# Forming a gating tile on VectorE instead of ScalarE in the mixing stage of a hybrid retention / SSD / MoE layer

## The reference

```python
def step(s, inp):
    xc, ac, bc, cc = inp                     # xc already holds dt * x
    acum = jnp.cumsum(ac, axis=1)
    seg = acum[:, :, None] - acum[:, None, :]
    lmat = jnp.exp(jnp.where(mask[None, :, :, None, None], seg, -jnp.inf))
    cb = jnp.einsum('bngs,bmgs->bgnm', cc, bc)
    y_in = jnp.einsum('bgnm,bnmgr,bmgrp->bngrp', cb, lmat, xc)
```

## Time and profile before

| | us |
|---|---|
| median of three runs (2853.01 to 2857.82) | 2855.8 |
| the profiled execution | 2853.01 |
| its span, first to last instruction | 2851.3 |
| TensorE busy in the span | 2332.4 |
| VectorE busy | 1407.6 |
| ScalarE busy | 1058.9 |
| GpSimd busy | 579.5 |

### The profile page before, as it was taken

One profiled execution on the slowest core, in us unless ns is written; L12 is line 12 of the kernel. 1 busy time (PEld: TensorE's weight loads), 2 busy tenths in 40 slices (PEclk: granted clock), 3 DMA queues, 4 the chain that ended last, 5 costly groups with the idle time before them and its releaser, 6 DMA issues. The chain is left out here.

```text
span 2851.3 us, 36459 instructions
## 1 busy us (share of the span) xinstructions
PE 2332.4 (82%) x11872; PEld 1917.0 (67%) x11873; DVE 1407.6 (49%) x1540; ACT 1058.9 (37%) x1471; POOL 579.5 (20%) x610
## 2 busy tenths in 40 slices
PE   4899989999994736787769991599999999999850
PEld 2688878999994315666658870477777777777740
DVE  2333331100102876788864444066566656546858
ACT  2333333222221220333322221166566656546732
POOL 0000000000001335677720014110010000000126
PEclk8899998999986869899989995699999999999985
DMA  7222241121115758544423433378696877658969
GB/s 257 70 89 88 88 151 64 45 89 44 45 62 169 293 198 306 212 157 162 162 84 140 147 117 98 118 261 292 226 319 240 279 266 248 222 201 292 362 223 372
DMA packets 296543, 517.35 MB, mean 181 GB/s; under 512 B 35248, under 2 KB 209456, under 8 KB 292272
## 3 DMA queue, kind: packets, MB, share of 16 engines
q1 hardware_dynamic: 261168, 394.52, 40.4%
q0 software_dynamic: 19200, 63.49, 6.4%
q10 hardware_dynamic: 16128, 58.73, 5.1%
HBM read 407.99 MB, written 108.69 MB: 181 GB/s over the span
## 5 line engine op out<-in xcount | busy, mean ns | idle before, releaser
L2107 DVE TENSOR_TENSOR e_w_low<-e_w_whole,e_w_high 128x2048 fp32r<-128x2048 f32 x186 | 417.9, 2288 | 128.8 <-ACT e_w_high L2060 128.8
L2060 ACT ACTIVATE e_w_high<-e_w_whole 128x2048 fp32r<-128x2048 f32 x186 | 345.5, 1908 | 44.8 <-DVE e_y L2125 44.8
L2013 PE MATMUL e_pG<-e_w_high,e_xT 128*128 128x512 f32 x768 | 305.3, 398 | 1.2 <-ACT e_xT L2053 1.2
L2014 PE MATMUL e_pG<-e_w_low,e_xT 128*128 128x512 f32 x768 | 305.5, 398 | 0.0
L602 PE MATMUL proj_acc<-w_high,hT_high 128*128 128x512 f32 x672 | 272.9, 406 | 6.9 <-DVE hT_low L637 5.7
L602 PE MATMUL proj_acc<-w_low,hT_high 128*128 128x512 f32 x672 | 268.7, 400 | 0.0
L602 PE MATMUL proj_acc<-w_high,hT_low 128*128 128x512 f32 x672 | 268.1, 399 | 0.0
L2032 PE MATMUL e_pY<-e_w_high,e_hT 128*128 128x512 f32 x768 | 226.0, 407 | 0.0
L2017 PE MATMUL e_pG<-e_w_high,e_xT 128*128 128x512 f32 x768 | 194.6, 395 | 0.0
L2013 PEld LDWEIGHTS e_pG<-e_w_high,e_xT 128*128 128x128 f32 x768 | 145.3, 189 | 36.6 <-issue 1.6
L2014 PEld LDWEIGHTS e_pG<-e_w_low,e_xT 128*128 128x128 f32 x768 | 145.4, 189 | 35.4
(11 more groups left out here) (286 smaller groups left out, 4509.5 us busy)
## 6 DMA issues: line engine op xcount, KB each, us to landing
e_w_whole<-in_moe_w_gate_dram SPq DMA_DIRECT2D x64, 1024.0 KB, 7.4
e_w_whole<-in_moe_w_up_dram SPq DMA_DIRECT2D x64, 1024.0 KB, 10.7
e_w_whole<-in_moe_w_down_dram SPq DMA_DIRECT2D x64, 1024.0 KB, 7.5
rows_done<-e_y ACTq DMA_DIRECT2D x48, 512.0 KB, 6.5
m_tok<-by_token SPq DMA_DIRECT2D x16, 1280.0 KB, 7.0
xt<-in_x_dram SPq DMA_DIRECT2D x32, 512.0 KB, 5.7
wm_rest<-in_w_mod_dram POOLq DMA_DIRECT2D x8, 2048.0 KB, 12.7
by_token<-tok SPq DMA_DIRECT2D x16, 768.0 KB, 5.6
```

The source lines that it names most:

```text
L2013: nc.tensor.matmul(pG[:, half], xT[:, 0, k], wh[:, half, w], start=(k == 0), stop=False)
L2014: nc.tensor.matmul(pG[:, half], xT[:, 0, k], wl[:, half, w], start=False, stop=False)
L2060: nc.scalar.activation(wh[:, third, part], raw[:, third, part], ACT.Copy).then_inc(whs.sem, 1)
L2107: nc.vector.tensor_tensor(wl[:, third, part], raw[:, third, part], wh[:, third, part].bitcast(F32), ALU.subtract).then_inc(wls.sem, 1)
```

## The change

The eight instructions that form `G` leave ScalarE and go to VectorE. On ScalarE each was an activation with a scale and a bias for each partition; on VectorE each is a `tensor_scalar`, multiply and add, with the same two operands. They stand behind `sT` (L1463) and ahead of the SSD output of tile t (L1467). The wait that ScalarE had for L1409 of the tile before falls away, since writer and reader are now on one engine in order. The counter `spreads` is gone; `gate` now counts three reports for each tile, the filling of `G` first.

```diff
-        spreads = kit.counter("m_steps_spread", 1)
-        gate = kit.counter("m_decays_gated", 2, credit=2)
+        gate = kit.counter("m_steps_spread", 3, credit=3)
...
-            def steps(t):
-
-                act.wait_ge(gate.sem, gate.at(t - 1, 1))
-                for h in range(SH):
-                    m = nc.scalar.activation(G[:, h], g["tri"][:, 0], ACT.Identity,
-                                             scale=g["dd"][:, bass.ds(t + NCT, 1), 0, h:h + 1].rearrange("p a b -> p (a b)"),
-                                             bias=g["dd"][:, bass.ds(t + NCT, 1), 1, h:h + 1].rearrange("p a b -> p (a b)"))
-                m.then_inc(spreads.sem, 1)
-
             def body(t, use, s):
                 if there(t + 1):
-                    steps(t + 1)
...
-                    dve.wait_ge(spreads.sem, spreads.at(t))
+                    dve.wait_ge(gate.sem, gate.at(t, 1))
                     dve.wait_ge(exps.sem, exps.at(t))
                     nc.vector.tensor_tensor(L[:], L[:], G[:], ALU.mult).then_inc(gate.sem, 1)
-                    dve.wait_ge(gate.sem, gate.at(t, 1))
+                    dve.wait_ge(gate.sem, gate.at(t, 2))
...
                     nc.vector.tensor_tensor(sT[:], bank[:, 4], g["DT"][:].rearrange("p h n -> p (h n)"), ALU.mult).then_inc(sTs.sem, 1)
+
+                    for h in range(SH):
+                        m = nc.vector.tensor_scalar(G[:, h], g["tri"][:, 0], g["dd"][:, bass.ds(tile, 1), 0, h:h + 1].rearrange("p a b -> p (a b)"),
+                                                    g["dd"][:, bass.ds(tile, 1), 1, h:h + 1].rearrange("p a b -> p (a b)"), ALU.mult, ALU.add)
+                    m.then_inc(gate.sem, 1)
```

## The result

The changed kernel takes 2875.8 us (median of four runs, 2873.1 to 2877.6) against 2854.9 (2853.0 to 2857.8): ratio 1.0069, 95% interval 1.0054 to 1.0084. It is slower by 20.9 us. The forecast was 2881, slower, with a range of 2862 to 2892.

The account below looks back on a forecast made before the run. The mixing loop was held to be bound by a cycle through the m_tok load, with VectorE idle at L1431. Adding 13.9, 9.9 and 2.2 us to 2853.0 gave 2879.0; the forecast was 2881, range 2862 to 2892.

Parts of the forecast that it names:

- The ring: Mixing loop: POOL's gate L1255, next loads, TensorE's transposes and L1317, VectorE's L1431, next L1255; 18.44 us a round.
- the spare: VectorE's idle time at L1431, behind load and TensorE: 40.1 us over 14 turns, 2.48 each in eleven.
- The removal at 0: Taking the eight activations, 3.19 us, off ScalarE gains 0, since nothing in the loop's cycle waits for them.
- The walk through the port: VectorE and POOL take turns on SBUF: the eight's 1.66 us of work becomes 3.82 us of delay up to L1409.
- The sum: Mixing loop's added time: 13.9 us up to L1431, 9.9 behind it, 2.2 in the last tile; 26.0 in all.
- first legs: From L1255's end to L1431, 10.84 us in the turn shown: 1.26 longer in eleven turns, 13.9 us.
- second legs: From L1431 to the next L1255's end: 8.31 us instead of 7.60, 0.71 in 14 turns, 9.9 us.
- long turns: Three loop turns with waits of 4.52, 4.16 and 4.11 us at L1431, said to lose nothing up to L1431.
- The port is not lost: Rival: the eight run in one go, 1.66 us; only the last tile pays, +2 us, 2855 to 2860; chance 0.12.
- Faster: Rival: the tile's store starts later, so m_tok lands 0.8 to 1 us sooner; 11 us gained, 2845; chance 0.05.
- Half of it: Rival: one POOL instruction misses the eight, or the way from L1431 does not stretch; 2862 to 2872; chance 0.18.
- More: Rival: two per-partition numbers make each instruction dearer, +0.3 to 0.8 us a turn; 2886 to 2895; chance 0.12.

Follow-up runs that it names:

- second execution: The kernel before, profiled again without any edit: 2854.7 us in a single run, loop 297.5 us.
- the half fill: The changed kernel with heads 0 to 3 of G on ScalarE and 4 to 7 on VectorE: 2862.3 us, ratio 1.0013 to the kernel before.
- the PSUM run: The changed kernel with the eight reading PSUM instead of SBUF, so G differs: 2839.0 us with one block of expert rows fewer; loop 298.9 against 316.4.
- the last experiment: The changed kernel with the eight moved into VectorE's idle stretch, behind L1426 and ahead of L1431: 2876.9 us, ratio 1.0077 to the kernel before.

## Why the prediction was right, and what was off

**The ring and the spare** held. Taking the load out of it gives back 33 us before, and nothing of the loop after.

**The removal at 0** held: 0.9994.

**The walk through the port** held to a quarter of a microsecond. It gave the eight 5.69 us (1.67 to 7.36), measured 5.93; L1409's end at 8.91 behind the gate, measured 9.13 (1272.19 + 1.21 − 1264.27); L1431 at 12.1, measured 12.1 to 12.2 in all fourteen turns. The order of the four waits was as written: the second to fifth of the eight take 1.06, 1.08, 1.08 and 1.93 us, the other four 0.33 to 0.34. The step was the small error: two per-partition numbers make 0.33 and 0.25 a step, not 0.29 and 0.207 (eight without company take 2.13 us for the first tile). Most of it hid behind POOL.

**The sum** of the loop against the first execution: first legs 14.2 us for 13.9 (14 x 12.21 = 170.9, before 156.8); second legs 9.9 for 9.9 (8.26 against 7.55 on average); the last tile 2.5 for 2.2 (its first leg 8.07 before, 10.53 after). 26.5 for 26.0. There is a little luck in the 14.2: the eleven short turns lost 15.2 and not 13.9, because L1409's end moved by 4.04 and not by 3.82, and the three long ones, which were to lose nothing, came out 1.0 shorter, since the changed kernel has no long turns. The stretch of the second leg, called one of the weakest steps, came out as the first tile had shown it.

**Where the 5 us between 26.5 and 20.9 lie** is in part open. The term that I hold to be off is the one for the long turns: the sum took their number, three, from one profile. The second execution of the kernel before has six and a loop of 297.5, so the change adds 18.9 to that one and 26.5 to the first. The changed kernel's loop is 316.4 and 316.5 in two profiles, since it no longer waits for what varies. One estimate speaks for a usual loop near that of the second execution: the half fill, whose turns are all alike, has a loop of 301.9 and runs some 4 us above the kernel before, which puts the latter's loop at 297 or 298. It is not shown: two profiles do not say how often long turns come, and the stretch ahead of the loop varies by 12 us by itself. I had also put the long turns down to the load alone; most of their length is TensorE's clock behind the wait.

**The rivals.** "The port is not lost" falls by the rows of the turn and by the PSUM run. "Faster" falls: the store now is issued 4.9 us later (8.2 us behind the gate instead of 3.3) and lands in 2.7 us instead of 7.0, but `m_tok` lands in 6.8 instead of 7.0, so 0.2 was there, not 0.8. "Half of it" did not happen. Its price for a turn without the `dav`, 8 to 12 us left in all, was too high: the run without it shows none (at most 2.3 by its interval). "More" was right that each instruction is dearer and wrong on how little of that hides: 0.24 us of a turn, not 0.3 to 0.8; its own terms give 2886 to 2893, not 2895. The Trainium skill's figure of 0.127 us for such an instruction (VectorE: DVE Perf Modes, TRN2 errata) is about half of the 0.25 step here. The Trainium skill's rule of the exclusive lock (SBUF — State Buffer, Who interferes with whom) agrees with the waits for `dav`, `kd`, `xd` and the decayed states in every run, and with the PSUM run; it does not with POOL's root of 4 columns in the last experiment, during whose 1.03 us VectorE's instructions ran at 0.34.

## What to carry to other kernels

Before giving VectorE work on SBUF, look at what GpSimd does in that stretch, not at VectorE's idle time: here a run of short instructions let each waiting large GpSimd instruction in between, and 2.13 us of work took 5.93. Reading PSUM avoided it even though each instruction got dearer. And where one engine has spare time because a ring passes through a load, try shortening the ring before filling the spare: here that was worth 33 us.

## What the runs showed of the hardware that I had not expected

- POOL gets the port between two VectorE instructions even when these follow at 0.25 us: in the last experiment the `dav` got in between the sixth and the seventh. In the changed kernel each of four POOL instructions (1.1, 1.0, 1.0, 1.9 us) had to be waited for by one of the eight.
- Not every POOL instruction is waited for: beside the root of 4 columns, 1.03 us long, VectorE's instructions kept their 0.34.
- A 512-column instruction of 0.47 us took 2.13 us when it met a `dav` (the half fill).
- In the two executions of the kernel before, TensorE's eight transposes took 1.6 to 2.0 us in eight turns, behind waits of 2.1 to 4.1 us, and 1.09 in the others, behind waits of 0.8 to 2.6: at 0.51 of the clock in the turn shown against full clock. The length of the wait alone does not tell which it will be.
